# A decode step on one Trainium2 core: a query row spread by the matmul engine, a reordered load list, two projection blocks moved around a maximum, and one set of sums of squares

## The reference

```python
u, q, k, v, f_logit, g_logit = split(rmsnorm(x) @ w_in)
x += (sig(g_pool) * (pool_mixer(u) @ w_up_pool) + sig(g_att) * (fox_attention(q, k, v, logf) @ w_up_att)) @ w_out
x += hier_moe(rmsnorm(x))        # 4 groups of 8 experts: best group, then best 2 experts in it
y = rmsnorm_final(x)
# the samples attend to pages of cache_k and cache_v that page_table names, with a softmax over all 1024 + 1 positions
```

## Time and profile before

| | |
|---|---|
| median of 3 runs | 713.39 us (712.56 to 715.01) |
| the profiled execution's own time | 715.12 us |
| its span in the trace | 713.3 us |
| mean granted TensorE clock | 0.912 |
| PE busy | 593.0 us (83%) |
| DVE busy | 214.7 us (30%) |
| ACT busy | 91.3 us (13%) |
| POOL busy | 52.2 us (7%) |
| DMA | 269.17 MB, 377 GB/s in the mean |
| chain that ended last | DMA 66%, PE 26%, DVE 4% |

### The profile page before, as it was taken

The page is one execution under the profiler, slowest core; times in us unless marked ns, Lnnn a source line. Parts: engine busy times, 40 slices in busy tenths (PEclk is TensorE's granted clock), DMA queues, the critical chain, the costliest instruction groups (busy, mean ns, idle before and its releaser), DMA issues.

```text
span 713.3 us, 13726 instructions
## 1 busy us (share of the span) xinstructions
PE 593.0 (83%) x6123; PEld 379.8 (53%) x6123; DVE 214.7 (30%) x523; ACT 91.3 (13%) x247; POOL 52.2 (7%) x58
## 2 busy tenths in 40 slices
PE   8999699999899989999776687767778767877883
PEld 7788577775488855545433344433444334443441
DVE  4159998852141252222111111111111111111113
ACT  3411234330000250000000000000000000000012
POOL 5135611022000000000000000000000000000000
PEclk9999899999999999999998889898889887898997
DMA  9996999966999869999999999999999999999982
GB/s 297 310 360 176 372 355 337 349 262 283 404 416 411 362 229 401 421 426 426 425 423 419 426 428 424 424 423 425 426 425 424 423 424 427 423 424 422 423 362 79
DMA packets 42403, 269.17 MB, mean 377 GB/s; under 512 B 9844, under 2 KB 10672, under 8 KB 23903
## 3 DMA queue, kind: packets, MB, share of 16 engines
q1 hardware_dynamic: 35616, 229.51, 80.3%
q0 software_dynamic: 3072, 35.19, 12.2%
q10 hardware_dynamic: 3655, 3.57, 1.5%
HBM read 266.02 MB, written 2.46 MB: 376 GB/s over the span
## 4 chain that ended last, share of the span: by engine, by line
DMA 66%; PE 26%; DVE 4%; issue 2%; ACT 1%; SPq 0%; DVEq 0%; POOLq 0%; ACTq 0%
DMA ring<-w_up 49%; DMA x<-w_up 6%; PE bank L1598 6%; DMA ring<-w_in 5%; PE bank L1657 4%; PE bank L1643 3%; DMA ring<-cache_v,ridx 2%; PE bank L1385 2%; DVE ring L1051 2%; DMA front<-q_scratch 1%; PE bank L1575 1%; PE bank L1494 1%; DMA q_scratch<-x 1%; PE bank L1485 1%; PE bank L1369 1%
## 5 line engine op out<-in xcount | busy, mean ns | idle before, releaser
L1385 PE MATMUL bank<-ring,front 128*32 128x256 f32 x1856 | 160.5, 484 | 85.4 <-DMA ring<-w_up 73.3
L1385 PEld LDWEIGHTS bank<-ring,front 128*32 128x32 f32 x1856 | 85.3, 138 | 145.8 <-issue 122.7
L1247 DVE COPY front<-bank 128x256 f32<-128x256 f32 x32 | 13.6, 425 | 232.6 <-PE bank L1385 232.6
L1598 PE MATMUL bank<-hT,ring 128*128 128x264 f32 x256 | 61.4, 396 | 7.0 <-DMA ring<-w_in 6.5
L1598 PEld LDWEIGHTS bank<-hT,ring 128*128 128x128 f32 x256 | 48.7, 194 | 17.5 <-DMA ring<-w_in 7.4
L876 ACT ACTIVATE front<-bank 128x128 f32<-128x128 f32 x32 | 8.9, 277 | 371.1 <-PE bank L1393 371.1
L1401 PE MATMUL bank<-ring,front 128*32 128x256 f32 x928 | 55.4, 379 | 0.0
L1369 PE MATMUL bank<-front 128*32 128x256 f32 (+1 forms) x768 | 52.9, 389 | 0.3 <-DVE front L1147 0.3
L1503 PE MATMUL bank<-hT,ring 128*128 128x264 f32 x192 | 44.3, 388 | 0.0
L1401 PEld LDWEIGHTS bank<-ring,front 128*32 128x32 f32 x928 | 30.0, 110 | 20.7 <-issue 1.1
L1257 DVE COPY front<-bank 128x256 f32<-128x256 f32 x32 | 13.6, 425 | 88.0 <-PE bank L1401 88.0
(11 more groups left out here) (312 smaller groups left out, 556.3 us busy)
## 6 DMA issues: line engine op xcount, KB each, us to landing
ring<-w_gate SPq DMA_DIRECT2D x28, 2048.0 KB, 14.8
ring<-w_up SPq DMA_DIRECT2D x28, 2048.0 KB, 14.7
ring<-w_down SPq DMA_DIRECT2D x28, 2048.0 KB, 14.7
ring<-w_in SPq DMA_DIRECT2D x8, 2048.0 KB, 24.1
x<-w_gate SPq DMA_DIRECT2D x3, 2048.0 KB, 14.7
x<-w_up SPq DMA_DIRECT2D x3, 2048.0 KB, 14.8
x<-w_down SPq DMA_DIRECT2D x3, 2048.0 KB, 14.8
ring<-w_out SPq DMA_DIRECT2D x2, 2048.0 KB, 20.0
```

The costliest lines, as they stand in the source:

```text
L1247: v.tensor_copy(gu.rearrange("p (c n) -> p c n", c=2), bank[GATEUP][:, 0:QUART].rearrange("p (n c) -> p c n", c=2)).then_inc(s_gusb, 1)
L1385: last = m.matmul(bank[GATEUP][32 * g:32 * g + 32, 0:256], xgT[:, k % 2, k // 2], w[:, k, 256 * (g % 2):256 * (g % 2) + 256], start=k == 0 ...
L1598: last = m.matmul(out[:, 0:TOK], w[:, k, cols], hT[:, k, 0:TOK], start=k == 0, stop=k == DK - 1)
```

## The change

Four edits. (1) Sample 0's query row no longer comes back from memory: a new step `qspread` has PE multiply a column of the 8x8 identity, broadcast to 128 columns, by the 8 query rows, and ACT copies the result from PSUM to `queries[0]`. SP issues only row 1 and waits only for row 1 before the router's loads; the rows still go to memory for the other samples. (2) `g` 0 is sorted ahead of `K` 2 in STREAM, which moves slots and waits of the loads behind it. (3) `gate` 14, `up` 0 and `up` 1 stand around `dmax`, the other `up` blocks close up behind, and `up` 1's load (`w_up_att`) also waits until `V` 6 has landed. (4) The squares of block 7 are added to `sqsum` too, and PE sums once. A fifth, small one: the first `turned(0)` of the router on DVE stands four operations earlier.

```diff
-        PLAN = Q[:2] + [("forget", 0)] + ... + U[:1] + [("nat", C_Q)] + U[1:3] + [("forgetT", 0)] + ...
+        PLAN = Q[:2] + [("forget", 0)] + ... + U[:1] + [("nat", C_Q)] + U[1:2] + [("qspread", 0)] + U[2:3] + [("forgetT", 0)] + ...
-        PLAN += [("m1", 0), ("gate", 13), ("dmax", 0), ("gate", 14), ("dshift", 0), ("gate", 15), ("dsums", 0)]
-        for b in range(NS):
-            PLAN += [("dpv", b)] + [("datt", 0)] * (b == 4) + [("up", b - (b >= 4))] * (b != 4)
-        PLAN += [("datt", 1), ("up", DK - 1)]
+        PLAN += [("m1", 0), ("gate", 13), ("gate", 14), ("up", 0), ("dmax", 0), ("up", 1), ("dshift", 0), ("gate", 15), ("dsums", 0)]
+        for b in range(4):
+            PLAN += [("dpv", b), ("up", b + 2)]
+        PLAN += [("dpv", 4), ("datt", 0), ("dpv", 5), ("dpv", 6), ("dpv", 7), ("up", DK - 2), ("datt", 1), ("up", DK - 1)]
-        STREAM = sorted(uses, key=lambda item: PLAN.index(uses[item][0]))
+        STREAM = sorted(uses, key=lambda item: PLAN.index(uses["K", 2][0]) - 0.5 if item == ("g", 0) else PLAN.index(uses[item][0]))
-        ready = {("q", b): PLAN.index(("nat", C_Q)) for b in range(2)}
+        ready = {("q", 1): PLAN.index(("nat", C_Q))}
-                for i in range(2):
-                    sp.wait_ge(s_qb[i], 16)
+                sp.wait_ge(s_qb[1], 16)
+                    if item == ("up", 1):
+                        sp.wait_ge(s_pages[where["V", NS - 2]], loaded["V", NS - 2])
+                elif step == "qspread":
+                    s.copy(queries[0], full("qspread")[:]).then_inc(taken[PART], 1)
+                elif step == "qspread":
+                    out = free("qspread")
+                    pe.wait_ge(*count_taken("natS", C_Q))
+                    m.matmul(out[:], ident8[:, 0:1].to_broadcast([NS, P]), samp[0:NS], start=True, stop=True).then_inc(filled[PART], 1)
+                        add_squares(DK - 1)
-                    pe.wait_ge(s_xsum, DK - 2)
-                    square_sums(logits, sqsum, False)
                     turned_logits(logits, DK - 1)
-                    pe.wait_ge(s_xsq, DK)
-                    square_sums(logits, sqc[:, (DK - 1) % 2], True).then_inc(filled[PART], 1)
+                    pe.wait_ge(s_xsum, DK - 1)
+                    square_sums(logits, sqsum).then_inc(filled[PART], 1)
```

More of the change, by code:

```diff
@@ L309, in build @@
         U, Q, K, V = (proj(c) for c in (C_U, C_Q, C_K, C_V))
-        PLAN = Q[:2] + [("forget", 0)] + Q[2:3] + [("fsum", 0)] + Q[3:] + [("pages", 0)] + U[:1] + [("nat", C_Q)] + U[1:3] + [("forgetT", 0)] + U[3:] + [("bias", 0)] + keys(0)[:2]
+        PLAN = Q[:2] + [("forget", 0)] + Q[2:3] + [("fsum", 0)] + Q[3:] + [("pages", 0)] + U[:1] + [("nat", C_Q)] + U[1:2] + [("qspread", 0)] + U[2:3] + [("forgetT", 0)] + U[3:] + [("bias", 0)] + keys(0)[:2]
         PLAN += K[:1] + keys(0)[2:3] + [("nat", C_U), ("psum", 0), ("psum", 1)] + K[1:2] + keys(0)[3:] + [("pool", 0), ("psum", 2)] + K[2:3] + keys(1)[:2] + K[3:] + keys(1)[2:] + [("psum", 3)]
@@ L382, in build @@
                 assign(CHAIN, step)
-            elif step == "forget":
-                assign(PART, "forget")
+            elif step in ("forget", "qspread"):
+                assign(PART, step)
             elif step == "bias":
@@ L1049, in run_plan @@
                         ks = wait_loaded(dve, "K", b).rearrange("p (j n) -> p j n", j=PAGES)[:, 2 * pair:2 * pair + 2]
-                        dve.wait_ge(s_qb[b % 3], 16 * (b // 3) + 16)
+                        if b:
+                            dve.wait_ge(s_qb[b % 3], 16 * ((b - 1) // 3) + 16 if b % 3 else 16 * (b // 3))
+                        else:
+                            dve.wait_ge(*count_taken("qspread"))
                         v.tensor_tensor(ks, ks, queries[b % 3].unsqueeze(1).to_broadcast([P, 2, DC]), ALU.mult).then_inc(s_kprod, 1)
@@ L1206, in route @@
                     link(v.tensor_tensor(ra, e, rankp, ALU.mult))
+                    if c == 0:
+                        turned(0, True)
                     link(v.tensor_reduce(rank[:, :, c], ra, AX.X, ALU.add))
@@ L1210, in route @@
                     link(v.tensor_tensor(wE, wE, selE[:, :, c, 1], ALU.add))
-                    if c == 0:
-                        turned(0, True)
                 v.tensor_tensor(selS, M["rank"][:, 0:CAP].unsqueeze(1).unsqueeze(1).to_broadcast([P, 3, 2, CAP]),
@@ L1343, in turned_logits, with square_sums @@
                     m.matmul(out[0:n, 36 * b:36 * b + 36], xT[:, c, b * P:b * P + n], wr[:, c], start=(b, c) == (0, 0), stop=False, skip_group_check=True)
-            def square_sums(out, src, last):
+            def square_sums(out, src):
                 for b, n in enumerate(rows_of):
-                    ins = m.matmul(out[0:n, 108 + b:109 + b], src[:, b * P:b * P + n], ones[:, 0:1], start=False, stop=last, skip_group_check=True)
+                    ins = m.matmul(out[0:n, 108 + b:109 + b], src[:, b * P:b * P + n], ones[:, 0:1], start=False, stop=b == 2, skip_group_check=True)
                 return ins
```

## The result

The change made the kernel 0.4% slower: 716.48 us in the median of 20 runs (711.79 to 719.68) against 714.75 us for 20 runs of the kernel before beside it, a ratio of 1.0041 with a 95% interval of 1.0026 to 1.0055. By the ratio that is +2.9 us (interval 1.9 to 3.9) where I had forecast -2.05; the two medians themselves lie 1.7 us apart. By either the kernel became slower, not faster. The profiled execution spans 717.2 us (before 713.3); its mean granted clock is 0.909 (before 0.912).

The account below looks back on a forecast made before the run. PE's work up to the slot used at 264 us was taken to bound the kernel. Terms -2.7 + 1.5 - 0.85 = -2.05 us gave a median of 711.3 us, range 706.8 to 716.0.

Parts of the forecast that it names:

- The bound: Start of the expert stretch: PE's use of a slot at 264.12 us sets it, so PE's gains move the end one for one.
- Query row: First `keys` product on DVE: starts at about 48.6, 2.7 us earlier; the new PE matmul costs at most 0.6 us.
- DVE's lead is worth nothing by itself: DVE ahead of `dmax`: `m1` ends at 151.98, 3.5 us before PE asks for it, so starting `keys` earlier gains nothing.
- `g` 0 and `K` 2, forecast -2.7: PE at the gates: with `g` 0 loaded ahead of `K` 2, gate 4 starts at 105.0 instead of 107.7, -2.7 us.
- the same sum for `g` 0 alone gives 81 to 89; I take 84: Landing of `g` 0 by queued bytes: taken as 84, a wait of 3 us behind PE's need at 81.0.
- it asks at 104.7 at the latest and stands for 0.3 us: PE ahead of gate 4: needs `g` 1 20.7 us after `g` 0, at 104.7, and waits 0.3 us.
- The time that I took for `g` 1, 105: Landing of `g` 1: the middle between 109.5 at 344 GB/s and 100.3 at 420 GB/s.
- Rival B: Gates: `K` 2 in front delays them, `g` 1 landing at 109.5 at 344 GB/s; +2.5, 715.9 us, chance 0.20.
- The `up` blocks, forecast +1.5: PE at `dpv` 7: gathers of `V` 4 to 7 start 3.96 us later, the held `w_up_att` gives -2.5; net +1.5 us.
- My -2.5 for the held `w_up_att`: Gathers of `V` 6 and 7: holding `w_up_att` until `V` 6 lands stops it sharing the engines; -2.5 us, bounds 0 and -2.7.
- rival C: Value gathers decide: `w_up_att` did not slow `V` 6 and 7, and the clock falls; +2.05, 715.4 us, chance 0.14.
- One set of sums, forecast -0.85: PE ahead of the router: one sum of squares runs from about 245.85 to 246.6; -0.85 us, bounds -0.4 and -0.9.

## Why the prediction was wrong

**The bound was right.** In all profiles the slot's release by PE opens the expert stretch, and a shorter way to it shortens the span: 264.12 gave a span of 713.3, 269.28 gave 717.2, 257.02 gave 704.8. From the slot to the end it is 447.8 to 449.6 us in all eighteen profiles, so one for one within 2 us.

**Query row.** Right where it is seen: `keys` 0 started at 49.02 (forecast 48.6) with no wait for memory, and the matmul disappeared. "DVE's lead is worth nothing by itself" left out one thing: `g` 1 goes out when DVE has used `K` 1, at 70.91 instead of 72.79, and that is where its earlier landing, by 1.4 us, comes from. The query row was never run alone, so its own worth isn't measured.

**`g` 0 and `K` 2, forecast -2.7: the steps "the same sum for `g` 0 alone gives 81 to 89; I take 84" and "it asks at 104.7 at the latest and stands for 0.3 us" failed.** I had put all traffic from `g` 0's issue on into one queue of bytes, with `g` 0 far back in it. But `g` 0 now goes out ahead of the gathers (at 55.41, earlier than my 58.4, since the router's loads were over sooner), and it landed 9.7 us later, at 65.1 and not at 84; in the thirteen profiles with this edit it took 9.3 to 13.0 us, in four without it 23.3 to 23.4. So `gate` 0 started at 81.42 instead of 86.45 and took 3.72 us instead of 5.35, PE asked for `g` 1 at 102.06, and a wait of 4.2 us arose where I had 0.3. `g` 1 itself was issued only 1.9 us earlier, and its transfer took 34.9 to 36.4 us in the nine profiles of these loads without the hold of `K` 6, and 34.8 to 35.2 in the kernels without the edits.

The time that I took for `g` 1, 105, was nearer. The sum of bytes was right: 17.64 MB went at 346 GB/s, where I had 17.6 MB and 344 GB/s from the trace and then took a middle between this pace and that of the expert stretch. From 55.41 on 17.6 MB at 344 GB/s end at 106.6; where PE waited for `g` 1, gate 4 started between 105.93 and 107.03, 1 to 2 us behind the forecast. Rival B had the pace right; its start at 58.4 was late.

Behind the wait the clock fell, which I had priced for `g` 0's wait and not for its successor: the 32 records took 7.39 us without the fall, 8.88 with 3.4 us at half and 10.02 with 6.8. What is left of the -2.7 can be read at the start of `gate` 13, ahead of every other edit. In the seven profiles that have both load edits and nothing else at `g` 1 it lies between 150.0 and 153.6, 151.6 in the mean; in the five without them between 151.8 and 152.1, 151.9 in the mean. That is a gain of 0.3 us in place of 2.7, which can't be told from none with a spread of this size, and the edits made the place vary by some 2 us either way.

Two loads of the same 2 MB, 9.7 us and 35.3 us: the second shares its time with page gathers. The traffic from 61 to 82 us in the changed kernel, by queue (packets, MB, share of the engines' time):

```profile
q0 software_dynamic: 369, 5.52, 66.4%
q1 hardware_dynamic: 632, 1.26, 16.7%
```

The gathers moved 5.52 MB in 66.4% of the engines' time, the gate weights 1.26 MB in 16.7%. By these rows a packet of the gathers, 15 KB on average, held one of the sixteen engines for 0.60 us on average, and one of the weights, 2 KB, for 0.09. No run changes the size of a packet, so whether this is why the gathers had more of the engines was not shown. What a run does show is that the gathers count: with one of them taken out of the stretch `g` 1 landed 4 us earlier and the time went down 0.82%. Its transfer was 5 to 7 us shorter, and 2.1 MB at 346 GB/s are 6.1 us, so a plain sum of bytes explains that too. That the gathers passed well I had written as a point for the earlier landing; by this run it counts for a later one.

**The `up` blocks, forecast +1.5: the wait was nearly right, the clock was left out of the likeliest case.** My -2.5 for the held `w_up_att` meant that `V` 7 lands 24.2 us behind the issue of `V` 4; without the hold the changed kernel shows that the hold is worth 2.0. `dpv` 7 starts 24.99 us behind that issue (before 26.71, so the hold gave 1.7 to 2.0 us and not 2.5). The issue is later by the 3.56 us of the two blocks and not by 3.96: +1.8 in all, against the +1.5 of the forecast. Behind it come falls of the clock: `dpv` 7 took 3.64 us instead of 1.92, and the way to the first `merge` 8.82 us (192.80 to 201.62) instead of 6.28 (190.92 to 197.20), +2.5. I had carried that as a bound (+5.6 with a fall of 1.6) and put it into rival C alone. The fall isn't there every time: of six profiles with a wait of 3.3 us and more that nothing covers, two have 6.8 us at half, three have 3.4 and one has none. With 3.4 the way to `merge` is 7.9 us, so that fall costs the 1.6 us that I had seen behind `g` 0. The dummies ahead of `dpv` 7 alone give it a price of 0.22%, 1.6 us, but the two intervals overlap (1.0002 to 1.0035 and 1.0026 to 1.0055), so zero is not excluded.

**One set of sums, forecast -0.85: right in the trace, not to be seen in the time.** From DVE's last addition of `out` (248.90) to the first use of the sums (251.15) the changed kernel takes 2.25 us, before it was 3.06 (244.48 to 247.54): -0.81. The router stretch behind it then varies by more. In the fourteen profiles with one sum, from its start to the used slot it is 16.0 to 16.1 us where no half clock is in it (three: the changed kernel's second profile, the one with dummies ahead of gate 4 alone, and the one with more dummies in this stretch), 17.4 to 17.6 with 3.4 us at half (five), 18.8 to 19.0 with 6.8 (six, the changed kernel's first among them): 1.5 us for each 3.4 us. Of the four with two sums, two have 17.4 with 3.4 us at half, and two have 16.2 and 16.3 though 3.4 us are at half, so the price depends on where the fall lies. The kernel before had 17.42, so 1.5 us of the 5.16 between the two profiles are a longer fall here. I can't say that this is no effect of the change: all six falls of 6.8 us are in kernels with one sum and none in the four profiles with two, which is too few to tell chance from a cost that eats the 0.8.

**The sum.** Of the first pair of profiles: up to `gate` 13 0.0, `V` 7 +1.8, the clock behind it +2.5, sums -0.8, the clock in the router stretch +1.6: +5.1 at the slot, where 5.16 are seen. Of the ratios: the load edits +0.05%, the `up` blocks with the hold +0.32%, the sums +0.02%, together 0.39% where the whole change measured 0.41%; each is known to 0.15 to 0.2%, so that the agreement is this close is luck. The forecast of -2.05 us missed by 5 us, known to 1 us: 2.4 in the gates, 0.3 in the landing of `V` 7, up to 2.5 in the clock behind it, and about 0.8 in the gain of the sums, which the times don't show. The measured time lies near those of rivals B and C (715.9 and 715.4), but neither came true: `g` 1 landed before 107.7, and `V` 7 not 26.7 us behind the issue of `V` 4. What remains open is the `up` blocks' share: taken out of the changed kernel they gave back 0.76%, added to the kernel before they cost 0.42% over the hold alone, each known to about 0.3%. The difference may be noise; whether the longer wait in the changed kernel (3.7 to 4.0 us against 3.3) and the clock behind it are part of it wasn't settled.

## What to carry to other kernels

A load that is brought forward moves the wait to the next load in the same crowded stretch. Ask of each load by itself what sets its issue and which transfers share its time: here one sum of bytes gave the landing of the last load to 1 or 2 us and missed the first one's by 19. Use the pace measured in that stretch, not a better one from elsewhere. Ask of every block that moves ahead of another which slot the latter frees; here 3.6 us of matmuls ahead of `gate` 15 delayed four gathers behind it. Where a gather is issued as soon as its slot is free but used 40 us later, let it wait for the load that is needed first: one such line gave 0.8%, and with the `up` blocks back 0.9% against the kernel before.

## What the runs showed of the hardware

- Executions of one kernel differ by several microseconds: 20 of the changed kernel took 711.79 to 719.68 us. Its two profiles differ for the most part through TensorE's clock: spans of 717.2 and 711.8 us, with 17 and 7 us at half clock up to 270 us (`g` 1's landing accounts for 0.3 us of it). In the router stretch of the kernels with one sum it was at half for 0, 3.4 or 6.8 us. There each 3.4 us cost about 1.5 us (16.0, 17.5 and 18.9 us for the stretch), and at most 0.3 us in two profiles with two sums where it fell early in the stretch. The 5.4 us between the two spans are 0.8% of one. Where the question is 0.3%, one profile of each kernel does not answer it, and a new wait of some 3 us needs a term for the clock in the sum: of the six uncovered waits of 3.3 to 5.2 us at `dpv` 7, five had 3.4 or 6.8 us of half clock with them.
- The same load of 2 MB took 9.3 to 13.0 us from issue to landing when it went out ahead of the page gathers, and 34.8 to 36.4 us when four or more gathers ran beside it.
- `K` 2, gathered into the crowded stretch, was awaited by DVE for 0.44 to 4.13 us in the profiles that have this edit, issued within 0.7 us of the same time, and PE then waited for DVE up to 2.4 us at 87 us. In the kernels that have no wait for `g` 1 this is what is late next: `V` 4 went out at 158.3 us with a wait of 1.05 us for `K` 2, and at 161.3 with one of 3.21.
